# Two half-height loads for the third and fourth contraction tiles of the first two weight blocks

## What is computed

```python
h = x
for layer in range(DEPTH):
    xn = rms_norm(h, norm_mix_g[layer])
    if layer % 2 == 0:
        proj = xn @ ab_w_in[j]
        u_pool, q, k, v = ...            # column ranges of proj
        mix = jnp.concatenate([y_a, y_b], axis=-1) @ ab_w_out[j]
    else:
        ...
    h = h + mix
    hn = rms_norm(h, norm_ffn_g[layer])
    h = h + (jax.nn.silu(hn @ ffn_w_gate[layer]) * (hn @ ffn_w_up[layer])) @ ffn_w_down[layer]
return rms_norm(h, norm_final_g)
```

## Time and profile before

| | us |
|---|---|
| median of 3 runs | 579.51 (579.14 to 580.39) |
| the profiled execution, its own time | 579.54 |
| span of the profile in it | 577.3 |
| PE busy in the span | 568.4 |
| DVE, ACT, POOL busy | 408.5, 278.6, 15.5 |

### The profile page before, as it was taken

One profiled execution on the slowest core, in us unless ns is written; L12 is line 12 of the kernel. 1 busy time (PEld: TensorE's weight loads), 2 busy tenths in 40 slices (PEclk: granted clock), 3 DMA queues, 4 the chain that ended last, 5 costly groups with the idle time before them and its releaser, 6 DMA issues.

```text
span 577.3 us, 8426 instructions
## 1 busy us (share of the span) xinstructions
PE 568.4 (98%) x3159; PEld 491.1 (85%) x3159; DVE 408.5 (71%) x546; ACT 278.6 (48%) x395; POOL 15.5 (3%) x55
## 2 busy tenths in 40 slices
PE   8999999999999999999999999999999999999995
PEld 7899988788888888888889999888888888888884
DVE  6579995775666777667777999767476666677753
ACT  6688665544343443444456345544444444344322
POOL 1200001000000000000000000000000000000000
PEclk9999999999999999999999999999999999999999
DMA  8986444463566645448468541623745446665401
GB/s 307 329 304 197 161 145 146 146 225 112 178 215 218 218 165 181 173 160 303 146 207 297 188 147 55 207 104 125 239 154 171 173 168 207 218 217 179 149 0 73
DMA packets 30408, 105.50 MB, mean 183 GB/s; under 512 B 3376, under 2 KB 4144, under 8 KB 30384
## 3 DMA queue, kind: packets, MB, share of 16 engines
q1 hardware_dynamic: 30096, 104.91, 53.2%
q10 hardware_dynamic: 288, 0.27, 0.2%
HBM read 104.11 MB, written 1.05 MB: 182 GB/s over the span
## 4 chain that ended last, share of the span: by engine, by line
PE 86%; DVE 4%; DMA 3%; issue 3%; SPq 2%; ACT 1%; POOL 0%; POOLq 0%; DVEq 0%; ACTq 0%
PE bank L1647 20%; PE bank L1251 17%; PE bank L1253 17%; PE bank L1252 17%; PE bank L1650 11%; DMA raw<-in_slabs 3%; DVE w_lo L776 2%; PE bank L1320 1%; PE bank L1419 1%; PE bank L1616 0%; SPq L331 0%; PE bank L1445 0%; PE bank L1406 0%; DVE h L824 0%; SPq L335 0%
## 5 line engine op out<-in xcount | busy, mean ns | idle before, releaser
L776 DVE TENSOR_TENSOR w_lo<-raw,w_hi 128x2048 fp32r<-128x2048 f32 (+2 forms) x95 | 211.4, 2227 | 20.8 <-ACT w_hi L444 20.8
L444 ACT ACTIVATE w_hi<-raw 128x2048 fp32r<-128x2048 f32 x91 | 173.2, 1910 | 11.4 <-DMA raw<-in_slabs 6.5
L1647 PE MATMUL bank<-xT,w_hi 128*128 128x512 f32 x512 | 128.0, 392 | 0.0
L1647 PEld LDWEIGHTS bank<-xT,w_hi 128*128 128x128 f32 x512 | 92.9, 189 | 17.2
L1251 PE MATMUL bank<-w_lo,yT_hi 128*128 128x512 f32 x240 | 95.5, 398 | 0.0
L1253 PE MATMUL bank<-w_hi,yT_lo 128*128 128x512 f32 x240 | 93.6, 390 | 0.0
L1252 PE MATMUL bank<-w_hi,yT_hi 128*128 128x512 f32 x240 | 93.6, 390 | 0.0
L1171 DVE TENSOR_REDUCE work<-bank 128x512 f32<-128x1024 f32 x32 | 39.0, 1220 | 77.0 <-PE bank L1650 77.0
L1650 PEld LDWEIGHTS bank<-xT,w_lo 128*128 128x128 f32 x512 | 69.8, 190 | 5.0
L1650 PE MATMUL bank<-xT,w_lo 128*128 128x256 f32 x512 | 71.4, 282 | 0.0
L689 ACT ACTIVATE work<-work 128x256 f32<-128x256 f32 x32 | 13.4, 419 | 97.2 <-DVE work L1171 97.2
(11 more groups left out here) (177 smaller groups left out, 595.0 us busy)
## 6 DMA issues: line engine op xcount, KB each, us to landing
raw<-in_slabs SPq DMA_DIRECT2D x186, 512.0 KB, 4.6
raw<-in_slabs SPq DMA_DIRECT2D x6, 256.0 KB, 5.6
h<-in_x SPq DMA_DIRECT2D x2, 512.0 KB, 8.0
gain<-in_norm_ffn_g SPq DMA_DIRECT2D x2, 512.0 KB, 7.2
out<-h SPq DMA_DIRECT2D x4, 256.0 KB, 2.0
raw<-in_slabs SPq DMA_DIRECT2D x4, 128.0 KB, 5.3
h<-in_x_cols SPq DMA_DIRECT2D x1, 512.0 KB, 5.6
gain<-in_norm_mix_g SPq DMA_DIRECT2D x1, 512.0 KB, 6.0
```

Of the source, the lines that this page charges most:

```text
L444: A(w_hi[:, t % SLOTS, :], raw[:, t % RAW_SLOTS, :], ACT.Copy).then_inc(hi_ready, 1)
L776: V.tensor_tensor(w_lo[:, t % SLOTS, c], raw[:, t % RAW_SLOTS, c], w_hi[:, t % SLOTS, c].bitcast(F32), ALU.subtract).then_inc(lo_ready, 1)
L1647: T.matmul(bank[:, b + m, :], hi, xT[:, k, :, :, :], start=k == 0, stop=False)
```

## The change

The third and fourth tile of blocks 0 and 1 (1024 floats per partition) are no longer loaded as one 128 x 512 piece and two 128 x 256 pieces. They are loaded as two pieces of 64 partitions x 1024 floats, that is with 4 KB rows: partitions 0 to 63, then 64 to 127. Both raise `raw_loaded[s]`. The split of the third tile on ACT now waits for that semaphore at 32, which is what the split of the fourth waits for. The load of x columns 2 and 3 stays directly behind tile 1.

```diff
-                for p in range(FIRST_PARTS):
+                for p in range(2):
                     c = slice(p * 512, (p + 1) * 512)
-                    sp.dma_start(raw[:, s, c], slabs[s, :, c]).then_inc(first_loaded[FIRST_PARTS * s + p], 16)
-                    if s == 0 and p == 1:
-                        sp.dma_start(x_rest[:, 2:4, :], cols_of[:, 2:4, :]).then_inc(cols_loaded[2], 16)
-                for c0 in range(FIRST_PARTS * 512, SLAB, 256):
-                    sp.dma_start(raw[:, s, c0:c0 + 256], slabs[s, :, c0:c0 + 256]).then_inc(raw_loaded[s], 16)
+                    sp.dma_start(raw[:, s, c], slabs[s, :, c]).then_inc(first_loaded[2 * s + p], 16)
+                if s == 0:
+                    sp.dma_start(x_rest[:, 2:4, :], cols_of[:, 2:4, :]).then_inc(cols_loaded[2], 16)
+                for r in (slice(0, P // 2), slice(P // 2, P)):
+                    sp.dma_start(raw[r, s, SLAB // 2:], slabs[s, r, SLAB // 2:]).then_inc(raw_loaded[s], 16)
                 if s == 0:
                     sp.dma_start(x_rest[:, 4:KC, :], cols_of[:, 4:KC, :]).then_inc(cols_loaded[3], 16)
...
                 if s < FIRST_SLABS:
-                    act.wait_ge(first_loaded[FIRST_PARTS * s + p], 16)
+                    act.wait_ge(*((first_loaded[2 * s + p], 16) if p < 2 else (raw_loaded[s], 16 * LOADS)))
```

More of the change, by code:

```diff
@@ L211, in trunk @@
         raw_loaded = [sem(f"raw_loaded{i}") for i in range(RAW_SLOTS)]
-        first_loaded = [sem(f"first_loaded{i}") for i in range(FIRST_SLABS * FIRST_PARTS)]
+        first_loaded = [sem(f"first_loaded{i}") for i in range(FIRST_SLABS * 2)]
         hi_ready = sem("hi_ready")
```

## The result

| | before | changed |
|---|---|---|
| median of 6 runs, us | 580.05 (579.14 to 580.47) | 582.33 (581.64 to 583.12) |
| span of the profile, us | 577.3 | 579.4 |

The ratio is 1.0039, with a 95% interval of 1.0028 to 1.0049: the changed kernel is 0.39%, or 2.3 us, slower. The forecast was +0.4 us and the range ended at 581.5 us; the time is that of rival B (+2.3 us).

What follows compares the result with a forecast made beforehand. Loads were taken to bind the start, PE everything behind 52 us. 579.5 us plus 0.4 for slower loads (+0.20 per block), with fewer issues at nothing and the third-tile stall swallowed, gave 579.9 us; range 579.0 to 581.5 us.

Steps and rivals of the forecast that it cites:

- rival B: Pairs of blocks 0 and 1: half the partitions, half the rate; up to +1.15 us per block, 581.8 us; chance 0.25.
- What bounds the start: Loads bind the first 52 us and nothing behind; a shift of the load queue at block 2 stays in the total.
- PE's three waits: L1303 (block 2), L1311 (norm's scale rows), L1419 (first attention weights): about 0.4 us each, all set by the load queue.
- D: Time the load queue runs late or early at block 2, kept in the total: 2e, forecast +0.40 us.
- Part 1: Price of the half-height loads in blocks 0 and 1: between -0.12 and +1.15 us per block, taken as +0.20.
- e: Extra load time per block in blocks 0 and 1 from the half-height form; forecast +0.20 us.
- The slow end: Upper bound for the half-height loads: half rate, 205 GB/s, no overlap with the partner, 2.55 us, +1.15 us per block.
- part 2: One issue of 0.43 to 0.71 us fewer per block; hidden by the queue, costed at nothing.
- Part 3: Third tile waits for both loads: PE stalls 0.4, 0.7 or 1.65 us in block 0, none in block 1.
- Part 4: At L1303 of block 2 the wait for the load swallows the third-tile stall, so the total shifts by 2e.
- Rival A: Row size is all that counts: half-height loads run at the 4 KB rate; -0.24 us, 579.3 us; chance 0.27.

Runs made afterwards that it cites:

- the join: Against the changed kernel: third and fourth tile of blocks 0 and 1 come as two 128-partition loads with 2 KB rows; 580.35 us against 580.37 for the kernel before.
- the one load: Against the changed kernel: one 128-partition load with 4 KB rows for both tiles in blocks 0 and 1; 580.81 us against 580.37 for the kernel before.

## Why the prediction was wrong

**What bounds the start** was right in the main. Loads bind until block 2, and most of what the queue loses there is paid for in the total. That PE's three waits are one thing, all shifted by the same D, was wrong for L1311: its scale rows came 1.4 us later, not 2.7, and the wait vanished. The granted clock is 1.00 in every stretch shown.

**Part 1 is the step that failed**, with the value taken between its two bounds. I took e = +0.20 us per block, a quarter of the way from full rate, because the long time from issue to landing let me think that the DMA engines need not be in step and that some would write upper partitions while others write lower ones. The rates show no such overlap. The slow end had 205 GB/s and +1.15 us per block; the runs showed 236 and 248 GB/s in the changed kernel, 226 in the run with halves in all later blocks, and +2.3 us for both blocks. The time from issue to landing says how much is queued, not that the engines are at different places in the queue. The loads of a pair landed 1.6 and 1.7 us apart, which fits engines that take the lower half and then the upper half nearly together; no row shows where each engine stood. The row that would have served was the DMA share of over 1.0, which leaves no idle time in which a slower load could hide. I used it in part 2 and in rival B but not for this price, and gave the rival 0.25.

That the total is rival B's +2.30 us to the tenth is in part luck. B's price was for 205 GB/s; the 226 that was sustained gives 524 / 226 - 1.40 = 0.92 us per block, 1.84 us for both. Block 2 was taken 2.4 to 2.9 us later than in the join, the one load and the even and odd partitions, and 0.6 us of the shift was then given back. In the changed kernel the rate is low for longer than the two pairs' own bytes need at 226 GB/s (4.6 us): it is 242 to 326 GB/s from 7 to 10 us and 229 to 293 from 11 to 15. So neighbouring loads seem to be slowed as well; this was not measured apart.

The Trainium skill, SBUF — State Buffer, section "Door 1: The DMA port swizzle", had the direction and nearly the size: its 196 against 328 GB/s is a ratio of 0.60. Here 236 against 391 GB/s from 12 to 14 us is 0.60 as well, and 226 against 410 is 0.55. The page's map of partitions to ports, in which bit 6 of the partition picks one of two, agrees with these runs: partitions 32 to 95 gave back half of the loss, and even and odd partitions all of it. The ports themselves are in no trace. What the Trainium skill says on the same page in the section "Can I just issue two DMAs to hit both halves?", that two such loads serialize, agrees with the two halves here. Its sentence there that "The only way to hit all 16 ports is one transfer spanning all 128 partitions" does not fit the measurement, as pairs of 64 ran at 406 to 416 GB/s, the rate of full-height loads.

**Part 2** (an issue less is worth nothing) fits: in the run with even and odd partitions, which has the same eight issues, the time is that of the kernel before.

**Part 3** had the right mechanism and, even for the slow end, too early a time: both tiles there at 9.32 us, PE near 10.0; ACT took the third tile at 10.05 us and PE at 10.82. Part of PE's delay was there before the third tile: its second tile began at 7.93 us in place of 6.98, as x columns 2 and 3 came late. Their load, which stands ahead of the half-height loads in the queue, landed 6.0 us after its issue:

```profile
h<-in_x_cols SPq DMA_DIRECT2D x1, 256.0 KB, 6.0
```

against 4.7 us before. I had taken the loads ahead of the changed ones as untouched. The same load took 5.5 us in the second execution of the kernel before, 5.4 in the join, 6.0 with one load of 4 KB rows and 5.7 with even and odd partitions, so half-height loads are not needed for it, and part of it differs from execution to execution. For block 1 I had said that there is no stall; at the slow end's 14.5 us there would have been none, and with ACT at 15.58 there was a short one, 0.2 us.

**Part 4** was right in its mechanism: the stalls at the third tiles are taken in by the wait at block 2, and the join alone costs nothing that can be measured. That nothing gives D back was wrong by about 0.6 us: 2.70 at block 2 became 2.1 in the span.

**Rival A** failed for lower and upper halves. With all partitions, or with even and odd ones, the rate is that of the 4 KB stretch (406 to 418 GB/s), but no gain reached the end, and 2 KB rows ran as fast in the join. **Rival B** is what happened, in its place and nearly at its price. **The range** took B up to three quarters of its price and ended at 581.5 us; with the upper bound of the unknown cost in it, as it should have been, it would have reached 581.8 (580.05 + 2.30 = 582.35 us from the median of all six runs before; 582.33 was measured).

## What to carry to other kernels

When a change cuts a load by partitions, ask first which partitions each piece writes: here two loads of 64 ran at 236 to 248 GB/s as lower and upper half, and at 406 to 416 as even and odd. Where the DMA share is at 1.0 and the next wait of the main engine hangs on that queue, a slower load is paid nearly in full (here 2.1 of 2.70 us), and an estimate from "they may overlap" needs a row that shows the overlap. The join of two waits ahead of a later wait on the same queue cost nothing measurable here; look at the later wait before pricing the first.

## What the runs showed of the hardware

- The loss is in the time that packets take: the DMA share stays at 1.03 and 1.04 while the rate falls from 397 and 391 to 248 and 236 GB/s. A DMA share near 1.0 thus doesn't say that the rate is the highest possible.
- Loads of the lower and the upper 64 partitions that follow each other in one queue hardly fill each other's gaps: 226 GB/s over whole blocks, and behind 52 us a DMA share of 0.76 for 174 GB/s, where even and odd partitions need 0.45 for 154.
- Loads of 64 partitions are not slow as such: as even and odd partitions they move 406 to 416 GB/s.
- Rows of 2 KB written to the lower and the upper half of the partitions lost about half as much as rows of 4 KB (block 2 at 16.59 and 17.98 us; 15.56 for 2 KB rows at full height). The source was read in another order as well, and the reason is open.
